# Attention: copies of every second group of transposed weights on DVE between the scans, with a semaphore of their own

## The reference

```python
def stick_breaking_attention(x, w_qkv, w_out):
    """A[t,s] = sigmoid(z_ts) * prod_{s<j<t} (1 - sigmoid(z_tj)), s < t; o_t = sum_s A[t,s] v_s."""
    qkv = (x @ w_qkv).reshape(bn, s, 3, B_HEADS, B_HEAD_DIM)
    ...
    for blk in range(s // Q_BLOCK):
        ...
        z = jnp.einsum('bthd,bshd->bhts', qb, kb).astype(jnp.float32) * scale
        causal = s_pos < t_pos
        log_keep = jnp.where(causal, jax.nn.log_sigmoid(-z), 0.0)
        survive = lax.cumsum(log_keep, axis=log_keep.ndim - 1, reverse=True) - log_keep
        a = jnp.where(causal, jnp.exp(jax.nn.log_sigmoid(z) + survive), 0.0)
        outs.append(jnp.einsum('bhts,bshd->bthd', a.astype(vb.dtype), vb))
    ...
```

## Time and profile before

| | |
|---|---|
| median of 3 runs | 2722.66 us (2720.82 to 2723.33) |
| the profiled execution's own time | 2723.14 us |
| its span in the profile | 2721.4 us |
| PE, PEld busy | 2543.8 us (93%), 2152.2 us (79%) |
| DVE, ACT, POOL busy | 1482.9 us (54%), 1028.4 us (38%), 1113.1 us (41%) |
| mean granted TensorE clock | 0.977 |
| attention, from the first scores to the last output part | 1577.6 to 1942.5 us |
| groups of the change: ACT copies to `aT` (L1622) | 160, of which 96 of 512 columns and 64 of 384 |

### The profile page before, as it was taken

How to read it: one execution, slowest core, us unless ns; L and a number is a source line. 1 busy time by engine, 2 the same in 40 slices (tenths; PEclk the granted TensorE clock), 3 DMA queues, 4 the chain that set the end, 5 groups by cost and what they waited for, 6 DMA issues and landing times.

```text
span 2721.4 us, 35430 instructions
## 1 busy us (share of the span) xinstructions
PE 2543.8 (93%) x13100; PEld 2152.2 (79%) x13100; DVE 1482.9 (54%) x1959; ACT 1028.4 (38%) x1507; POOL 1113.1 (41%) x716
## 2 busy tenths in 40 slices
PE   7998999998999989999899978888997999989997
PEld 7997888876888868887898857776896888768886
DVE  3214655657656577776311135555348655577775
ACT  5222212234444333334211157777335444333332
POOL 2221221136555465554222144444235555465554
PEclk9999999998999989999999989999999999989999
DMA  5222121142544464443224544334122544464443
GB/s 163 93 92 93 63 70 54 62 133 77 169 151 157 141 229 149 157 171 124 94 93 155 185 116 109 92 92 100 47 80 95 171 151 147 163 231 139 139 166 120
DMA packets 180417, 342.56 MB, mean 126 GB/s; under 512 B 12224, under 2 KB 95168, under 8 KB 178240
## 3 DMA queue, kind: packets, MB, share of 16 engines
q1 hardware_dynamic: 173632, 311.47, 35.0%
q10 hardware_dynamic: 6656, 29.36, 2.7%
HBM read 235.95 MB, written 104.86 MB: 125 GB/s over the span
## 4 chain that ended last, share of the span: by engine, by line
PE 81%; DVE 7%; ACT 4%; issue 4%; POOL 3%; DMA 2%; SPq 0%; ACTq 0%; DVEq 0%; POOLq 0%
PE psum L1117 22%; PE psum L1160 20%; PE psum L934 13%; PE psum L921 12%; PE psum L945 5%; PE psum L1248 3%; DVE stick L2084 2%; PE psum L1218 2%; PE psum L1235 2%; ACT psum L1614 1%; PE psum L1038 1%; ACT brk L1608 1%; POOL rw_lo L878 1%; DMA a_raw<-a_forms 1%; DVE acc L1691 1%
## 5 line engine op out<-in xcount | busy, mean ns | idle before, releaser
L1160 PE MATMUL psum<-rw_hi,ra_hi 128*128 128x512 f32 x896 | 353.8, 395 | 17.4 <-POOL rw_lo L878 8.9
L1160 PE MATMUL psum<-rw_lo,ra_hi 128*128 128x512 f32 x896 | 352.1, 393 | 0.0
L1160 PE MATMUL psum<-rw_hi,ra_lo 128*128 128x512 f32 x896 | 351.6, 392 | 0.0
L791 POOL TENSOR_TENSOR w_lo<-stage,w_hi 128x1024 fp32r<-128x1024 f32 x56 | 134.2, 2419 | 507.5 <-ACT w_hi L1305 507.5
L878 POOL TENSOR_TENSOR rw_lo<-blk,rw_hi 128x512 fp32r<-128x512 f32 x160 | 239.7, 1528 | 196.1 <-ACT rw_hi L1446 196.0
L2084 DVE TENSOR_TENSOR_SCAN stick<-psum,brk 128x128 f32<-128x128 f32 (+7 forms) x128 | 173.4, 1356 | 161.2 <-ACT psum L1614 159.7
L894 POOL TENSOR_TENSOR brk<-brk,stick 128x128 f32<-128x128 f32 (+7 forms) x128 | 153.4, 1208 | 222.2 <-DVE stick L2084 208.6
L1441 ACT ACTIVATE ra_hi<-a_raw 128x2048 fp32r<-128x2048 f32 x56 | 107.3, 1917 | 357.7 <-PE psum L1160 259.4
L1971 DVE TENSOR_TENSOR ra_lo<-a_raw,ra_hi 128x512 fp32r<-128x512 f32 x224 | 230.9, 1040 | 19.9 <-ACT ra_hi L1441 19.9
L934 PE MATMUL psum<-w_hi,hT_hi 128*128 128x256 f32 x768 | 219.8, 286 | 1.4 <-DVE hT_lo L2091 1.4
L934 PE MATMUL psum<-w_lo,hT_hi 128*128 128x256 f32 x768 | 218.6, 285 | 0.0
(11 more groups left out here) (225 smaller groups left out, 6402.4 us busy)
## 6 DMA issues: line engine op xcount, KB each, us to landing
a_raw<-a_forms SPq DMA_DIRECT2D x56, 1024.0 KB, 5.5
a_forms<-a_out SPq DMA_DIRECT2D x64, 512.0 KB, 3.1
blk<-mlp_w_in SPq DMA_DIRECT2D x32, 1024.0 KB, 5.4
a_forms<-a_out SPq DMA_DIRECT2D x32, 768.0 KB, 3.3
stage<-a_w_in_in SPq DMA_DIRECT2D x16, 1024.0 KB, 5.4
stage<-mlp_w_in SPq DMA_DIRECT2D x16, 1024.0 KB, 6.0
raw<-mlp_w_in SPq DMA_DIRECT2D x32, 512.0 KB, 5.3
x_res<-xt SPq DMA_DIRECT2D x24, 512.0 KB, 4.9
```

Of the source, the lines that this page charges most:

```text
L791: pool.tensor_tensor(w[b][1][:, c], raw[:, c], w[b][0][:, c].bitcast(F32), ALU.subtract).then_inc(unit_ready, 1)
L1160: mm = pe.matmul(psum[:, down_bank(n, tp), :], ring_a[n % 3][sa][:, k, tp * P:(tp + 1) * P], ring_w[n % 3][sw][:, k, :], start=(p in (1, 2 ...
```

## The change

Every group with an odd `gi` is copied by DVE instead of ACT, and counts on a semaphore of its own, `aT_odd_in`; the even ones stay on ACT and on `aT_in`. Odd are, in each head, group 0 of pair 1, groups 0 and 2 of pair 3, and groups 0 and 2 of pair 2: five of ten, two of 512 columns and three of 384, in all 80 of the 160. DVE does them at the same places g of its list at which ACT did them, each in front of the scan of that place. PE's waits for a copy go to the semaphore of the group they mean.

```diff
         aT_in = sem("aT_in")
+        aT_odd_in = sem("aT_odd_in")
...
+        def keys_copied(eng, i, gi):
+
+            sem_, per = (aT_odd_in, GH) if gi % 2 else (aT_in, GH)
+            wait(eng, sem_, i * per + gi // 2 + 1)
...
-                wait(pe, aT_in, i * (2 * GH) + (gi - 1))
+                keys_copied(pe, i, gi - 2)
...
-                pe.wait_ge(aT_in, i * (2 * GH) + (groups_before(n) + g + 1))
+                keys_copied(pe, i, groups_before(n) + g)
...
             def keys_in(i, n, g):
+                if (groups_before(n) + g) % 2:
+                    return
...
+            def keys_in(i, n, g):
+                gi, c0 = groups_before(n) + g, P if g == 0 else 0
+                if gi % 2 == 0:
+                    return
+                dve.wait_ge(aT_psum, i * (2 * GH) + (gi + 1))
+                wait(dve, av_done, i * (2 * GH) + groups_before(n - 1))
+                dve.tensor_copy(aT[n % 2][:, g * HALF + c0:(g + 1) * HALF],
+                                psum[:, 4 + gi % 2, c0:HALF]).then_inc(aT_odd_in, 1)
...
                     for g in range(4):
+                        if g <= pair(n):
+                            keys_in(i, n, g)
                         if more and g % 2 == 0:
                             sticks(i, 2 * n + 4 + g // 2)
```

## The result

| | before | after |
|---|---|---|
| median of 5 runs | 2723.33 us (2720.82 to 2726.33) | 2736.45 us (2734.93 to 2738.36) |
| the profiled execution's own time, its span | 2723.14, 2721.4 us | 2736.45, 2734.7 us |
| DVE, ACT, POOL busy | 1482.9, 1028.4, 1113.1 us | 1525.6, 999.6, 1113.5 us |
| attention ends (first PE work of the output projection) | 1942.57 us | 1955.67 us |

The account below looks back on a forecast made before the run. A loop through all engines, none of them full, was taken to set the pace, 21.56 us a head. The terms -0.35 + 0.9 + 0.8 = +1.35 us on 2722.66 us gave 2724.0 us, range 2719.5 to 2729.

Parts of the forecast that it names:

- What leaves the chain: nothing.: Steady heads: the chain's one ACT copy, half a microsecond a head, stays on ACT; relief of ACT is worth nothing.
- DVE's prices: Each copy moved to DVE takes 0.682 us for 512 columns and 0.57 us for 384, 49 us over the attention.
- First pass: First pass of the attention: ACT's last even copy and the weight conversion start earlier, once -0.35 us (0 to -0.4).
- Last pass: Last pass: PE's pair 2 begins later, behind DVE's copies of groups 0 and 2, once +0.8 us (0 to +1.0).
- The tight copy: Copy of group 2 of pair 3, in PE's gapless run: +0.06 us a head, +0.9 over fifteen (0 to +3.0).
- In front of the scan of 640: DVE's copy ahead of that scan: DVE is still free 1.3 us before the scan of 768, so no cost.
- rival B: Waits hidden in PE's 11.5 us run shrink as scans come earlier: up to 5.6 us faster, 2718 us, chance 0.08.
- Group 0 of pair 3, and groups 0 and 2 of pair 2: These three copies on DVE: the first fits with 0.25 us to spare, the other two have no cost.
- Rival A: DVE copies wait for POOL products at group 0 of pair 3: 5 to 10 us slower, chance 0.12.

Follow-up runs that it names:

- e5: The kernel before with only the copy of group 1 of pair 1 moved from ACT to DVE: 2709.30 us, ratio 0.9938.
- e3: The kernel before with only the copy of group 2 of pair 3 moved from ACT to DVE: 2726.21 us, ratio 1.0010.
- e6: The changed kernel with the copy of group 2 of pair 3 put back on ACT: 2734.65 us, ratio 1.0032.
- e1: The changed kernel with the copy of group 0 of pair 1 put back on ACT: 2724.32 us, ratio 1.0004.
- e2: The kernel before with only the copy of group 0 of pair 1 moved from ACT to DVE: 2734.55 us, ratio 1.0044.
- e7: The kernel before with ACT's copy of group 0 of pair 1 behind the keep of 640 columns, nothing on DVE: 2734.40 us, ratio 1.0032.
- e4: The changed kernel with six unread matmuls of 256 columns a head ahead of the scores of 256 columns: 2728.03 us, ratio 1.0007.

## Why the prediction was wrong

The forecast was 2724.0 us and no change; it is 13 us above the kernel before and above the range. By its own steps:

- **What leaves the chain: nothing.** Right. The ACT copy of gi = 2 is still there, the chain from break 1024 to the scores of 256 columns is 10.0 us as before, and 42.5 us less copying on ACT bought nothing there. The half microsecond a head put on that one copy was too small: moving it alone (e5) gave 0.93, since the transposes ahead of it leave the chain too.
- **DVE's prices.** Right: 0.691 and 0.547 us against 0.682 and 0.57.
- **First pass**, -0.35 us. ACT's last copy and the conversion behind it come as forecast, after:

```profile
1604.13 0.60 ACT L1630 ACTIVATE aT<-psum 128x512 f32<-128x512 f32 x1 [0.47 <-PE psum L1241]
1604.62 1.91 ACT L1311 ACTIVATE w_hi<-stage 128x2048 fp32r<-128x2048 f32 x1
```

  The conversion begins 0.48 us earlier than in the earlier trace rows, and the second pass 0.29 us earlier.
- **Last pass**, +0.8 us. Right: +0.86 measured, by the steps forecast. The chain there, after: `out_lo`, the copy of group 0, the transposes of group 2, the copy of group 2, and pair 2 behind it, released by DVE and not by POOL:

```profile
1944.10 0.66 DVE hT_lo L2108
1944.76 0.47 DVE aT L2100
...
1945.28 0.67 PE psum L1241 x4
...
1945.98 0.70 DVE aT L2100
1946.68 0.14 issue
1946.81 0.52 PE psum L1241 x3
```

- **The tight copy**, +0.06 us a head, bounds 0 to 0.20. The mechanism was right and the size was off: 0.16 us in the changed kernel, 0.19 to 0.20 alone (e3), 0.14 to 0.16 when taken away (e6), and no more than 0.11 beside the three later copies (e1). After:

```profile
1744.19 0.69 DVE L2100 COPY aT<-psum 128x512 f32<-128x512 f32 x1 [0.65 <-PE psum L1241]
...
1744.79 0.10 PEld L1226 LDWEIGHTS psum<-mask_bf,ident_bf 128*128 128x128 bf16 x1 [0.16 <-issue]
...
1745.00 0.31 PEld L1241 LDWEIGHTS psum<-ident,brk 128*128 128x128 f32 x3
```

  The copy ends at 1744.88 and the load follows 0.12 us later; ACT's ended at 1741.36 and the load followed by 0.05. The copy is 0.09 us longer and the time from its end to the load 0.07 us longer, together 0.16. Only the first of the two is the same everywhere: in e1 the load follows DVE's copy by 0.05 us, in e3 too, but there the copy starts 0.09 us later, counted from the break of 1024 columns. The forecast went below the copy's own 0.09 because the scan of 256 columns no longer stands behind ACT's copy, and no kernel shows a head that costs less than that. 13 heads: 2.1 us where 0.8 was put for them.
- **In front of the scan of 640. "No cost."** This is the step that failed. It asked one question, whether that scan could be late, and found 1.3 us to spare. In fact the scan and the scores of 128 columns are early, by 0.25 and 0.08 us in turn. The working for the groups of pair 2 does note that keeps come earlier when ACT has no copy between break and keep, and counts it as harmless, and rival B as a possible gain. Earlier was not harmless. The forecast gave the scores of 128 columns until 1738.40 and so took PE's idle time as slack whose total alone matters; that total, 2.23 us, did not change. Its division did, from 0.61 + 1.62 and 0.43 + 1.80 to 0.37 + 1.86. With that, PE's granted clock fell to 1.2 GHz for 3.4 us of the run behind the idle time in seven heads of 13, which cost 1.44 to 1.59 us each, 10.4 us in all: a cost for which the sum has no term. Undoing the copy takes it away (e1), the copy alone brings it (e2), a mere reordering of ACT's list brings it (e7), and work put into the idle time takes it away with all copies in place (e4). The Trainium skill, "TensorE: Matmul & The Clock Gate", "A second HAM failure mode: psum-queue depth-cycling", tells of a kernel in which frequent short idle times of PE between groups of matmuls make the clock gate swing between its two levels, so that throughput is lost to the falls and returns. The trace agrees in kind: with idle times of 0.37 and 1.86 us in each head of 21.7 us, the granted clock of a head is 0.93 or 1.00. I had read the clock of the earlier trace rows, 1.00, as a property of the kernel rather than as one of the things that the change could move.
- **Group 0 of pair 3, and groups 0 and 2 of pair 2.** Right: in e1, with all four later copies on DVE, the heads are 0.10 to 0.11 us longer than before, no more than the tight copy's price.
- **Rival A.** It had the right side, 5 to 10 us slower where 13 were measured, but by the wrong mechanism. POOL's products take as long as before, 1.207 us in the mean against 1.208, after:

```profile
L900 POOL TENSOR_TENSOR brk<-brk,stick 128x128 f32<-128x128 f32 (+7 forms) x128 | 153.3, 1207 | 235.0 <-DVE stick L2092 221.5
```

  and no DVE copy is stretched: those of 512 columns take 0.667 to 0.691 us in the mean in every kernel that has them, those of 384 take 0.534 to 0.557. **Rival B** fell too: the scans came earlier and no head became shorter for it.

A small slip in the prediction's range has no part in this: 2722.66 + 4.0 and the 0.67 us by which the highest run lay above the median give 2727.3, where it has 2727.5.

What stays open is why seven of 13 heads fall and not all. The length of the idle time alone does not sort them. Heads with 1.86 us keep their clock in all four kernels that have seven slow ones; one head with 1.81 us (e3) and one with 1.80 (the last of e6) fall, while the six heads with 1.80 us of the kernel before do not. Nor is it chance: in e2, e6 and e7 the same seven of the 13 fall, the 3rd, 5th, 6th, 8th, 10th, 11th and 13th (in the changed kernel the 3rd, 4th, 6th, 7th, 9th, 11th and 12th). And the clock does not fall with the idle time but 0.5 to 1.5 us after PE has resumed, in all 29 falls of the five kernels, and stays down for 3.4 us each time. So something besides its length must matter, perhaps when in time it comes; this was not tested. Nor was it tested whether it is the length of the one idle time or all that PE does around it that counts; e4 changed both. And the kernel before, whose runs lie between 2720.2 and 2729.9 us, was profiled once: whether its slower runs hold such a head or two was not seen.

## What to carry to other kernels

Move the operation that stands on the chain, and not those that happen to be easy to alternate: one copy of ten gave 0.6%, while five others, off the chain, cost 0.5%. In a kernel in which TensorE waits in every period, an earlier start of a small piece of its work is not free by itself, since it can make the idle time behind it longer at the cost of the one ahead; look at the granted clock of each period and not only at its mean, and ask of a change there where the work will lie in the wait. If the pause can't be shortened, matmuls whose result nobody reads may pay inside it: here a microsecond of them in each of 16 heads was worth eight in all.

## What the runs showed of the hardware that was not expected

- With idle times of 1.62 and 1.80 us in turn ahead of PE's run, all 13 steady heads stayed at the full clock level. With 1.86 us, seven of 13 went to 1.2 GHz for 3.4 us each, in four kernels, and came back within the same run; each fall cost 1.44 to 1.59 us by the heads of the changed kernel. Single heads with 1.80 us (e6) and 1.81 us (e3) fell as well, so these runs give no sharp limit.
- The clock fell 0.5 to 1.5 us after PE had resumed work, not during the idle time.
- 1.06 us of matmuls whose result nobody reads, put into that idle time, gave back 9.6 us of the attention by the profiles and 8.4 by the medians, and cost nothing in the steady heads.
- DVE's copy of 512 columns took 0.69 us where ACT's took 0.60. PE's load followed its end by 0.12 us in the changed kernel and by 0.05 in e1 and e3, and ACT's by 0.05.
